# Columns handed to all partitions by transposes with step zero, and two nearly empty weight panels with two products instead of three

## The reference

```python
# first block
u = rmsnorm(h, norm_mix)                     # x * rsqrt(mean(x*x)) * gain, per token
proj = u @ w_in                              # [1024, 2824]: the last 8 columns are b (4) and a (4)
beta = sigmoid(b); g = -exp(a_log) * softplus(a + dt_bias)
g = cumsum(g) within a chunk                 # per token and head
decay = exp(g[:, None] - g[None, :])         # lower triangle, enters L and a_qk of the delta rule
...                                          # attention, delta rule, w_o, mlp, gate
h1 = rmsnorm(h, norm_final)
# second block, on 16 meta tokens and h1 (1040 tokens)
proj = rms_norm(h1, ln_w_2) @ w_in_2         # 12 parts; one of them, k_rope, is 32 columns wide
...                                          # convolution, retention, latent attention, w_out_2
```

## Time and profile before

| | us |
|---|---|
| median of 3 runs (1996.83 to 1999.29) | 1997.28 |
| the profiled execution | 1998.73 |
| its span, first to last instruction | 1996.9 |
| what lies around the span | 1.8 |
| PE busy | 1914.4 (96%) |
| weight loads of PE busy | 1566.2 (78%) |
| DVE busy | 1200.0 (60%) |
| ACT busy | 801.1 (40%) |
| POOL busy | 559.5 (28%) |
| mean granted clock of PE | 0.982 |

### The profile page before, as it was taken

One profiled execution on the slowest core, in us unless ns is written; L12 is line 12 of the kernel. 1 busy time (PEld: TensorE's weight loads), 2 busy tenths in 40 slices (PEclk: granted clock), 3 DMA queues, 4 the chain that ended last, 5 costly groups with the idle time before them and its releaser, 6 DMA issues.

```text
span 1996.9 us, 24294 instructions
## 1 busy us (share of the span) xinstructions
PE 1914.4 (96%) x9489; PEld 1566.2 (78%) x9489; DVE 1200.0 (60%) x1794; ACT 801.1 (40%) x1418; POOL 559.5 (28%) x561
## 2 busy tenths in 40 slices
PE   8999999989988999999999999989999999899999
PEld 6778888866766888887788887878988897677687
DVE  4477544455588676668777788446435348566641
ACT  5666222255553333333333344442111136455521
POOL 0041014740165655630000023651523134111100
PEclk9999999999998999999999999999999999899999
DMA  5143432211223445459655511123101314311133
GB/s 154 43 130 113 129 89 81 94 52 43 75 85 127 153 137 174 134 199 391 245 201 194 185 43 28 46 56 127 43 22 43 106 51 144 107 32 33 42 93 98
DMA packets 226186, 216.76 MB, mean 109 GB/s; under 512 B 37320, under 2 KB 166600, under 8 KB 225560
## 3 DMA queue, kind: packets, MB, share of 16 engines
q1 hardware_dynamic: 226072, 215.21, 33.5%
HBM read 154.31 MB, written 60.87 MB: 108 GB/s over the span
## 4 chain that ended last, share of the span: by engine, by line
PE 77%; DVE 12%; ACT 5%; POOL 3%; DMA 2%; issue 2%; SPq 0%; DVEq 0%; POOLq 0%; ACTq 0%
PE ps L337 11%; PE ps L338 10%; PE ps L339 10%; PE ps L1802 4%; PE ps L1804 4%; PE ps L2181 4%; PE ps L1803 4%; PE ps L2183 4%; PE ps L2182 4%; PE ps L350 4%; PE ps L3500 3%; PE ps L577 2%; PE ps L3401 1%; DVE fm L990 1%; PE ps L3489 1%
## 5 line engine op out<-in xcount | busy, mean ns | idle before, releaser
L337 PE MATMUL ps<-xh,whi 128*128 128x512 f32 (+2 forms) x1216 | 485.8, 399 | 9.5 <-DVE wlo L323 4.9
L338 PE MATMUL ps<-xl,whi 128*128 128x512 f32 (+2 forms) x1216 | 464.9, 382 | 0.0
L339 PE MATMUL ps<-xh,wlo 128*128 128x512 f32 (+2 forms) x1216 | 464.5, 382 | 0.0
L337 PEld LDWEIGHTS ps<-xh,whi 128*128 128x128 f32 x1216 | 232.7, 191 | 59.0 <-issue 10.3
L339 PEld LDWEIGHTS ps<-xh,wlo 128*128 128x128 f32 x1216 | 232.1, 191 | 41.6
L338 PEld LDWEIGHTS ps<-xl,whi 128*128 128x128 f32 x1216 | 233.0, 192 | 36.8 <-issue 2.6
L1802 PE MATMUL ps<-oph,wsh 128*128 128x512 f32 x448 | 176.9, 395 | 15.1 <-DVE stu L1914 6.5
L2181 PE MATMUL ps<-dnh_b,dnh_a 128*128 128x512 f32 x448 | 175.8, 393 | 6.9 <-DVE dn_b L2207 6.9
L1804 PE MATMUL ps<-oph,wsl 128*128 128x512 f32 x448 | 175.8, 392 | 0.0
L1803 PE MATMUL ps<-opl,wsh 128*128 128x512 f32 x448 | 175.7, 392 | 0.0
L2183 PE MATMUL ps<-dnh_b,dn_a 128*128 128x512 f32 x448 | 175.6, 392 | 0.0
(11 more groups left out here) (499 smaller groups left out, 3451.4 us busy)
## 6 DMA issues: line engine op xcount, KB each, us to landing
dnr_b<-ff_d SPq DMA_DIRECT2D x28, 1024.0 KB, 8.2
dnr_a<-w_down SPq DMA_DIRECT2D x28, 1024.0 KB, 5.6
wraw<-w_in SPq DMA_DIRECT2D x47, 512.0 KB, 3.9
ff_d<-st SPq DMA_DIRECT2D x64, 256.0 KB, 5.1
ff_d<-stt SPq DMA_DIRECT2D x48, 256.0 KB, 5.0
upx<-w_up SPq DMA_DIRECT2D x16, 512.0 KB, 4.3
upy<-w_up SPq DMA_DIRECT2D x16, 512.0 KB, 5.5
xt<-x SPq DMA_DIRECT2D x8, 512.0 KB, 7.7
```

The lines of the kernel that those rows point to most:

```text
L337: pe.matmul(out, h, xh[:, xk, c0:c1_], start=(n == 0), stop=False)
L338: pe.matmul(out, h, xl[:, xk, c0:c1_], start=False, stop=False)
L339: mm = pe.matmul(out, l, xh[:, xk, c0:c1_], start=False, stop=(n == nk - 1))
```

## The change

Four edits.

1. `pe_spread` takes the place of the products with ones. A transpose is a matmul of PE in which the data is the stationary operand and the identity moves past it; here the data is one column with a step of zero, read as a 128 x 128 matrix, and its transpose has the column as a row on every partition. Four transposes of 128 x 128 take the place of one float32 matmul of 128 x 512. The 14 diagonals go (2 and 4 on DVE, 8 on POOL), and the waits on them become waits on the columns.
2. Where a panel is nearly empty (NARROW: ba and kr), DVE writes the low part of its few columns into empty columns of the high panel, and PE makes two products in each step instead of three (`pe_narrow`). High and low sums come out on different partitions. For ba they are added after the turn: one more DVE operation for each half. For kr the nine transposes become nine products with `fold`, two identities of 32 added up (one small POOL operation makes it), which turn and add.
3. ACT takes all eight squares of x after the split of panel 1.
4. ACT and POOL wait for PE's R1 rows where they waited for the last diagonal.

```diff
+NARROW = {IN0: (slice(120, 128), slice(112, 120)), IN20 + 19: (slice(0, 32), slice(32, 64))}
...
+            if i in NARROW:
+                high, low = NARROW[i]
+                r, h = raw[b][:].rearrange("p (k n) -> p k n", k=8), whi[b][:].rearrange("p (k n) -> p k n", k=8)
+                dve.tensor_tensor(h[:, :, low], r[:, :, high], h[:, :, high].bitcast(F32), ALU.subtract).then_inc(*dve_w.up(i))
+                return
...
+    def pe_narrow(pe, w, done, key, i, emptier, x, ready, cols=HALVES, behind=None, every=4):
...
+                both = whi[buffer[i]][:, 128 * k:128 * k + 128]
+                pe.matmul(out, both, x[0][:, k, c0:c1_], start=(k == 0), stop=False)
+                mm = pe.matmul(out, both, x[1][:, k, c0:c1_], start=False, stop=(k == 7))
...
+    def pe_spread(pe, out, cols, c0):
+
+        return pe_turn(pe, [(out[:, 128 * j:128 * j + 128], bc(cols[:, c0 + j:c0 + j + 1], [128, 128])) for j in range(4)])
+
...
-            if hf == 1 and k % 2 == 1:
-                square(k // 2)
         act_split(act, w, 1)
-        for b in range(4, NB):
+        for b in range(NB):
             square(b)
...
-            w.wait_ge(*dve_x.at("diag", hf))
-            pe.matmul(p, ones[:], dgx[hf][:].rearrange("p b s -> p (b s)"), start=True, stop=True).then_inc(*pe_in.up("input norm", hf))
+            w.wait_ge(*dve_x.at("norm"))
+            pe_spread(pe, p, rx, 4 * hf).then_inc(*pe_in.up("input norm", hf))
...
-            w.wait_ge(*pool_in.at("diag", i))
-            pe.matmul(p, ones[:], Dgs[i % 2][:].rearrange("p h s -> p (h s)"), start=True, stop=True).then_inc(*pe_in.up("g", i))
+            w.wait_ge(*dve_in.at("gcum"))
+            pe_spread(pe, p, gcum, 4 * i).then_inc(*pe_in.up("g", i))
...
-                    dve.tensor_copy(ba[:, bs, :], bank4(tile("turn", kind, j, hf))[:, :, 120:128]).then_inc(*dve_in.up("turned", kind, j, hf))
+                    dve.tensor_copy(ba[:, bs, :], bank4(tile("turn", kind, j, hf))[:, :, 120:128]).then_inc(*dve_in.up("copied", kind, j, hf))
+                    w.wait_ge(*dve_in.at("copied", kind, j, hf))
+                    dve.tensor_tensor(ba[:, bs, :], ba[:, bs, :], bank4(tile("turn", kind, j, hf))[:, :, 112:120], ALU.add).then_inc(*dve_in.up("turned", kind, j, hf))
...
-                    w.wait_ge(*dve_i2.at("diag", which, hf))
                     p = take(w, "misc", (which, hf), (act_i2, (which, hf)))
-                    pe.matmul(p, ones[:], dgp[which, hf][:].rearrange("p h s -> p (h s)"), start=True, stop=True).then_inc(*pe_i2.up(which, hf))
+                    w.wait_ge(*dve_i2.at("qr" if which == "RST" else "r"))
+                    pe_spread(pe, p, cols8, (8 if which == "RST" else 0) + 4 * hf).then_inc(*pe_i2.up(which, hf))
...
-                w.wait_ge(*dve_i2.at("diag", "R1", 1))
+                w.wait_ge(*pe_i2.at("R1", 1))
...
-                    pe_turn(pe, [(p[0:key_block(x)[0], 32 * x:32 * x + 32], fkr[0:32, key_block(x)[1]]) for x in range(NB + 1)]).then_inc(*pe_la.up("turn kr"))
+                    w.wait_ge(*pool_la.at("fold"))
+                    for x in range(NB + 1):
+                        t = pe.matmul(p[0:key_block(x)[0], 32 * x:32 * x + 32], fkr[:, key_block(x)[1]], fold[:], start=True, stop=True)
+                    t.then_inc(*pe_la.up("turn kr"))
...
+        pool.tensor_tensor(fold[:], ident[:, 0:32], ident[:, 32:64], ALU.add).then_inc(*pool_la.up("fold"))
```

More of the change, by code:

```diff
@@ L322, in dve_split @@
             b = buffer[i]
-            dve.tensor_tensor(wlo[b][:, 0:n], raw[b][:, 0:n], whi[b][:, 0:n].bitcast(F32), ALU.subtract).then_inc(*dve_w.up(i))
+            if i in NARROW:
[3 more added lines that the diff above has]
+                return
+            dve.tensor_tensor(wlo[b][:, 0:n], raw[b][:, 0:n], whi[b][:, 0:n].bitcast(F32), ALU.subtract).then_inc(*dve_w.up(i))
+    def pe_narrow(pe, w, done, key, i, emptier, x, ready, cols=HALVES, behind=None, every=4):
+        for c0, c1_ in cols:
+            out = take(w, "dense", (*key, c0), (emptier, ("ev", *key, c0)))[:, 0:c1_ - c0]
+            w.wait_ge(*dve_w.at(i))
+            for k in range(8):
+                for ev in ready(k, c0):
+                    w.wait_ge(*ev)
+                both = whi[buffer[i]][:, 128 * k:128 * k + 128]
+                pe.matmul(out, both, x[0][:, k, c0:c1_], start=(k == 0), stop=False)
+                mm = pe.matmul(out, both, x[1][:, k, c0:c1_], start=False, stop=(k == 7))
+                if k == 7:
+                    mm.then_inc(*done.up(*key, c0))
+                if k % every == every - 1 and behind:
+                    behind()
+            weight_used[i] = done, (*key, c0)
     def pe_dense(pe, w, done, key, i, emptier, x, ready, nk=8, cols=HALVES, tl=0, step=128, behind=None, every=4, kind="dense", order=range(8), place=range(8)):
@@ L358, in build @@
     sqj = [M(f"sqj{i}", 64 + 4 * i, [T]) for i in range(2)]
-    dgx = [M(f"dgx{i}", 72 + 2 * i, [4, 128]) for i in range(2)]
     rx = sm["rk"][:, 0:8]
@@ L433, in input_norm_dve @@
         dve.reciprocal(rx, rx).then_inc(*dve_x.up("norm"))
-        w.wait_ge(*dve_x.at("norm"))
-        w.wait_ge(*ld_id.at())
-        for hf in range(2):
-            dve.tensor_tensor(dgx[hf][:], id4, bc(rx[:, 4 * hf:4 * hf + 4].unsqueeze(2), [128, 4, 128]), ALU.mult).then_inc(*dve_x.up("diag", hf))
     def stats_pe(pe, w, done, key, acc, ready, emptier, kind="misc"):
@@ L1073, in project_pool @@
                 turned(*in_panels[i - 1])
-            if i == 4:
-                for n in range(2):
-                    delta_pool(pool, w, "diag", n)
             if i == PREP0:
@@ L2385, in build @@
     PP = pH, pL = M("pH", 64, [2, T], F32R), M("pL", 72, [2, T], F32R)
-    dgp = {key: M(f"dgp{i}", kb, [4, 128]) for i, (key, kb) in enumerate(((("RST", 0), 42), (("RST", 1), 44), (("R1", 0), 36), (("R1", 1), 38)))}
     gts = [M(f"gts{i}", 48 + 2 * i, [512]) for i in range(4)]
@@ L2698, in final_stats_dve @@
         r, q = cols8[:, 0:8], cols8[:, 8:16]
-        def diag(col, which):
-            for hf in range(2):
-                dve.tensor_tensor(dgp[which, hf][:], id4, bc(col[:, 4 * hf:4 * hf + 4].unsqueeze(2), [128, 4, 128]), ALU.mult).then_inc(*dve_i2.up("diag", which, hf))
         w.wait_ge(*act_i2.at("sums"))
```

28 lines of the change are left out of this document (11 added, 17 removed).

## The result

The changed kernel took 1981.55 us (median of 4 runs, 1980.19 to 1981.96) and the kernel before, on the same chip, 1997.05 (median of 4, 1996.24 to 1999.29). The ratio is 0.9923 with a 95% interval of 0.9911 to 0.9935. On another chip it was 0.9930, 0.9918 to 0.9943, from 5 runs against 21 (1981.63 against 1996.02). So the change gains 14.4 to 15.5 us by the medians; the second interval alone reaches from 11.4 to 16.4. The forecast was a gain of 12.25 and a time of 1985.0.

A forecast was written before the change was run, and what follows sets the result against it. PE was taken as the bound, busy 96% of the span. Gains of 3.95 + 4.05 + 1.7 + 2.55 = 12.25 us from 1997.28 gave 1985.0 (1983 to 1987.5 at 0.62; 8 in 10: 1981.5 to 1991).

The forecast's parts named there:

- (b): Panel 0: 16 matmuls fewer at 0.227 us each, a gain of 3.63 us.
- (d): End of panel 1: the norm comes late because the squares stand last, a charge of 0.3 us, up to 2.
- (a): Panel 0: the DVE split shrinks from 1024 elements to 64, a gain of 0.2 us.
- (c): The two norm rows: transposes replace products with ones, 1.72 less 0.87, a gain of 0.85 us.
- (e): Chain from the norm to the SiLU: two added additions lengthen PE's wait, a loss of 0.45 us.
- g rows: Preparation, 97 to 170 us: eight spreads, 2.15 us for blocks 3 to 7 plus 1.9 for 0 to 2: 4.05.
- norms of block 1: 1360 to 1372 us: four spreads gain 1.7 us; the diagonals leaving DVE give nothing.
- kr: 1612 to 1652 us: fewer matmuls gain 3.8 us, fold products cost 1.26, a gain of 2.55.
- Third: Rival: PE falls to 1.2 GHz in the first half of panel 0, 8.6 us lost, 1993.6 us; chance 0.06.
- fourth: Rival: step-zero loads are slow at the 14 spreads, kernel slower than before, 2007 us at 2 us each; chance 0.05.
- The first: Rival: waits replace gain at norm, preparation and kr, 3.6 us less, 1988.6 us; chance 0.18.
- The second: Rival: preparation chain gives all of 2.5, shorter SiLU wait saves half of 6 us at half clock, 1981.5; chance 0.09.

The follow-up runs named there:

- changed_again: The changed kernel profiled and timed once more with no edit: 1981.63 us, 0.9930 of before.
- before_again: The kernel before, profiled once more with no edit: one run, span 1992.1 us.
- pool_diag: The changed kernel with POOL's eight diagonals of g put back as dead work, read by nobody: 1986.63 us, 0.9953 of before.
- narrow: The kernel before with only ba and kr in two products; diagonals, products with ones and squares between units kept: 1992.08 us, 0.9976 of before.

## Why the prediction was right, step by step

| step | forecast | measured | from |
|---|---|---|---|
| panel 0 up to the norm, (b) and (d) | 3.33 | 3.4 to 3.9 | 22.3 against 18.9 (both begun at half rate), 18.5 |
| its split, (a) | 0.2 | 0.3 | idle of PE's loads for it: 0.27, 0.26, 0 and 0.73 with three products, none in the eight with two |
| norm to k0, (c) and (e) | 0.40 | 0.36 | 20.50, 20.14; parts 0.86 and -0.44 |
| g rows | 4.05 | 4.2 | 114.0, 109.85 |
| norms of block 1 | 1.7 | 1.69 | 12.05, 10.36 |
| the stretch behind kdt | none | 1.55 | 8.23, 6.68 |
| kr | 2.55 | 2.57 | 3.80 - 1.23 |
| sum | 12.25 | 14.1 to 14.6 | |

**The sum** held at every step that it has, within 0.6 us; what it left out is one place, where it took the clock to stay as it was. For block 1 the end of the measured stretch matters: the first dense matmul starts 3.03 us behind the first product with ones and 1.66 behind the first transpose, 1.37 less, but the second one follows 0.63 us behind the first there and 0.32 here. From the second on the difference is the forecast's 1.7. The delay at the norm, 0.57 us from start to start, was forecast at 0.3.

**The time** came out 3.45 us below the forecast. Part of it is the point it was counted from: 1997.28 was the median of three runs, 1996.2 is that of all 44 that there are by now: 1.1 us. The profile's own execution, 1998.73, was above both, and so the difference between the first two profiles, 17.5, overstates the gain. Of its 5.25 beyond the forecast, 1.6 are the stretch at the turn of k0 and 1.6 the one in kr and the sums ahead of it, both 6.8 us long before and 3.4 after, 1.4 the start of panel 0 (15.12 and 13.54, less the 0.2 of the forecast), and 1.55 the stretch behind kdt. One goes the other way, 1.6: behind the next wait, at 1505 us before and 1490 after, the clock was at 0.50 for 3.4 us before and 6.8 after. Over the whole span it was at 0.50 for 74 us before and 75 after, mean 0.982 in both, so the stretches that vary cancel in these two profiles. In changed_again and before_again they have the other lengths; the one behind kdt does not vary. The rest lies in pieces of at most 0.4 us. The steps of the table give 14.1 to 14.6 us and the medians (1996.2 and 1981.6) 14.6. So of the 3.45 us by which the time fell below the forecast, 1.1 are its starting point and 1.55 this stretch.

**The g rows** were right in size and too narrow in reason. From one g row to the next the changed kernel takes 1.03, 0.43, 1.04, 0.49, 0.41, 0.43 and 0.39 us less (before_again against changed). The last four are what PE saves by a spread, as I had said. The first three are 2.5 together, my upper bound, where I took 1.9: three spreads and 1.2 of PE's waits. The last block's own spread gives nothing to its L. I had counted five blocks as PE's and three as the chain's, and given back some of DVE's slowing only in those three. pool_diag shows that with the diagonals in place the other path is as long in the later ones too. Had the change spread the columns by transposes and left the diagonals on POOL for some other use, my arithmetic would have given 5 x 0.43 = 2.15 for blocks 3 to 7 and been wrong.

**The squares.** I said that a unit leaves ACT enough time once they are gone, and took from it that ACT bounded the rounds before. narrow shows that it didn't: rounds of 0.90 are there with the squares in place. It is the split of panel 1 that they made late.

**The rivals.** Third and fourth are refuted by rows. The first had its mechanism in part (0.41 for the reciprocal) and not its size. The second said 1981.5, and that is nearly the time. Its smaller half came (2.5 for blocks 0 to 2); the larger did not: PE's wait for the SiLU grew and the stretch at 0.50 behind it stayed, 3.4 or 6.8 us long with either kernel. Clock was won at another wait, 1400 us later, so that its number fits is luck.

## What to carry to other kernels

A cheap operation on the bounding engine gains only if the second path is shortened too: put the removed work of the other engines back as dead work, and see what is left of the gain. Before crediting a stage with what two profiles differ by, look at the length of its stretch at half clock in both, and profile each kernel twice. Here two stages looked 3.2 us better by it, and a third 1.6 worse. A stretch that is there in every profile of one kind and in none of the other, as the one behind kdt, counts to the change, even where what causes it stays open. Measure a stage up to a point where both kernels run alike again, not to the first matmul behind the edit. And an ACT queue that changes its table four times ahead of what PE waits for is worth a look: here, with the SiLU first and the two exp side by side, it was 3.4 us up to the end of the preparation, by one profile of each, about 1.6 of it the clock's.
